# The up projection of a 512-token block as seven products of quarters instead of eight, with the sums of weight quarters made beforehand in DRAM

## The reference, cut to what matters

```python
D_MODEL, SEQ, D_FF = 1024, 512, 4096
def first_block(x, ...):
    ...
    x = x + y @ w_out[l]
    xn2 = rmsnorm(x, norm2_g[l])
    x = x + jnp.square(jax.nn.relu(xn2 @ w_up[l])) @ w_down[l]
    return x
```

## Time and profile before

| | |
|---|---|
| median of 3 runs | 1969.43 us (1969.37 to 1969.91) |
| span of the profiled execution, first to last instruction | 1967.4 us |
| PE busy | 1959.2 us, 9686 matmuls |
| PE weight loads busy | 1614.8 us, 9686 |
| DVE busy | 1024.1 us |
| ACT busy | 764.9 us |
| POOL busy | 83.8 us |
| DMA | 183.36 MB, mean 93 GB/s |

### The profile page before, as it was taken

How to read it: one execution, slowest core, us unless ns; L and a number is a source line. 1 busy time by engine, 2 the same in 40 slices (tenths; PEclk the granted TensorE clock), 3 DMA queues, 4 the chain that set the end, 5 groups by cost and what they waited for, 6 DMA issues and landing times.

```text
span 1967.4 us, 23153 instructions
## 1 busy us (share of the span) xinstructions
PE 1959.2 (100%) x9686; PEld 1614.8 (82%) x9686; DVE 1024.1 (52%) x1394; ACT 764.9 (39%) x1226; POOL 83.8 (4%) x132
## 2 busy tenths in 40 slices
PE   9999999999999999999999999999999999999998
PEld 8888888888888888888888888888888888887776
DVE  5553466435453436643334355545554447596675
ACT  5556563332323333442134232222222321447864
POOL 0000000000000000000000000000000000005541
PEclk9999999999999999999999999999999999999999
DMA  6222222223122242233233323232323334521011
GB/s 214 84 68 85 65 86 75 86 91 106 65 91 86 87 148 86 86 107 108 86 105 89 106 86 107 86 107 89 105 86 107 86 124 114 152 81 44 23 55 65
DMA packets 184295, 183.36 MB, mean 93 GB/s; under 512 B 5120, under 2 KB 159232, under 8 KB 184192
## 3 DMA queue, kind: packets, MB, share of 16 engines
q1 hardware_dynamic: 179840, 172.15, 28.2%
q10 hardware_dynamic: 4352, 9.75, 1.6%
HBM read 175.59 MB, written 4.19 MB: 91 GB/s over the span
## 4 chain that ended last, share of the span: by engine, by line
PE 98%; ACT 1%; DVE 0%; DMA 0%; issue 0%; POOL 0%; DVEq 0%; ACTq 0%
PE bank L1403 85%; PE bank L1630 2%; PE bank L1611 2%; PE bank L1644 2%; PE bank L1501 1%; PE bank L1490 1%; PE bank L1529 1%; PE bank L1413 1%; ACT raw L1663 0%; PE bank L1464 0%; PE bank L1433 0%; PE bank L1509 0%; PE bank L1577 0%; PE bank L1446 0%; PE bank L1620 0%; PE bank L1431 0%
## 5 line engine op out<-in xcount | busy, mean ns | idle before, releaser
L1403 PE MATMUL bank<-xh,wh 128*128 128x512 f32 x1352 | 534.1, 395 | 0.0
L1403 PE MATMUL bank<-xh,wl 128*128 128x512 f32 x1352 | 527.6, 390 | 0.0
L1403 PE MATMUL bank<-xl,wh 128*128 128x512 f32 x1352 | 527.0, 390 | 0.0
L1680 ACT CAST wh<-raw 128x2048 fp32r<-128x2048 f32 (+2 forms) x151 | 279.5, 1854 | 408.8 <-PE bank L1403 405.1
L2234 DVE TENSOR_TENSOR wl<-raw,wh 128x2048 fp32r<-128x2048 f32 (+2 forms) x151 | 335.0, 2221 | 169.5 <-ACT wh L1680 169.3
L1403 PEld LDWEIGHTS bank<-xh,wl 128*128 128x128 f32 x1352 | 253.4, 187 | 53.8
L1403 PEld LDWEIGHTS bank<-xh,wh 128*128 128x128 f32 x1352 | 253.7, 188 | 50.3
L1403 PEld LDWEIGHTS bank<-xl,wh 128*128 128x128 f32 x1352 | 253.8, 188 | 50.0
L1403 PE MATMUL bank<-wh,xh 128*128 128x512 f32 x320 | 129.4, 404 | 0.0
L1403 PE MATMUL bank<-wh,xl 128*128 128x512 f32 x320 | 125.1, 391 | 0.0
L1403 PE MATMUL bank<-wl,xh 128*128 128x512 f32 x320 | 125.1, 391 | 0.0
(11 more groups left out here) (325 smaller groups left out, 2925.8 us busy)
## 6 DMA issues: line engine op xcount, KB each, us to landing
raw<-in_w_in SPq DMA_DIRECT2D x49, 1024.0 KB, 5.0
raw<-in_a_w_in SPq DMA_DIRECT2D x32, 1024.0 KB, 5.5
raw<-in_w_up SPq DMA_DIRECT2D x16, 1024.0 KB, 5.3
raw<-in_w_down SPq DMA_DIRECT2D x16, 1024.0 KB, 5.8
raw<-in_w_proj_b SPq DMA_DIRECT2D x8, 1024.0 KB, 5.1
raw<-in_a_w_out SPq DMA_DIRECT2D x8, 1024.0 KB, 5.7
raw<-in_w_out SPq DMA_DIRECT2D x4, 1024.0 KB, 5.2
raw<-in_w_kv SPq DMA_DIRECT2D x4, 1024.0 KB, 4.9
```

The lines of the kernel that those rows point to most:

```text
L1403: m = e.matmul(o, p, q, start=k == 0 and n == 0, stop=k == K - 1 and n == 2)
L1680: m = e.copy(hi, r)
```

## The change

**Seven products.** The work is cut into 8 groups (`f` 0 or 1, `g` 0 to 3) of 512 features. In a group the contraction is cut in two halves of 512 inputs, the features in two of 256 and the tokens in two of 256. The block product of 2 by 2 by 2 quarters has eight quarter products; here it is formed from seven, of sums of weight quarters and sums of activation quarters. A product (`seven`) is 2 feature blocks x 4 input blocks x 3 matmuls, each 128x128 stationary by 128x256 moving. Products 1, 6, 5 and 3 add up in one bank, `st12`; 2 has the bank `st11`; 7 and 4 share `st21`. On the way ScalarE copies `st12` to a `tmp` three times (`shot`, behind products 1, 6 and 5) and VectorE adds or subtracts the other bank (`piece_sum`); four pieces of 256 features by 256 tokens (two blocks of 128 features) come out. `SEVENS` is the order of the 28 products of a half.

**Weights.** Of seven weight operands three are plain quarters of `w_up`, four are sums. The sums lie in a new DRAM tensor `sums` (8 x 4 blocks of 128x1024). Pool makes them with 64 DMAs of 512 KB: 32 copies, 32 accumulating ones (`accum_op=ALU.add`), issued from the time when the first query tile is done, at most four in flight (four semaphores), each accumulation behind its copy. Loads for the products are 512 KB into halves of the `raw` buffers, six in all; splits (`part`) go to halves of the split buffers, four in all.

**Activations.** The four plain quarters and three sums of quarters of x are made in the stage of `w_out`, by VectorE in the buffer `between`; the sums that have no place in `xh`, `xl` go to the new tiles `xeh`, `xel`.

```diff
+SEVENS = [(0, 1), (1, 1), (2, 1), (0, 2), (1, 2), (0, 7), (1, 7), (0, 6), (1, 6), (0, 5), (1, 5), (0, 3), (0, 4),
+          (1, 3), (1, 4), (3, 1), (2, 2), (3, 2), (2, 7), (3, 7), (2, 6), (3, 6), (2, 5), (3, 5), (2, 3), (2, 4),
+          (3, 3), (3, 4)]
...
+def sevens(f):
+    out, low = [], []
+    for i, (g, n) in enumerate(SEVENS):
+        out.append(("seven", f, g, n))
+        if f == 0 and i == ROOT[1]:
+            out += [("sum_squares", 1), ("root", 1)]
+        out += low
+        if n in (2, 6, 5):
+            out.append(("shot", f, g, 1 if n == 2 else n))
+        if n in PIECE_OF:
+            out.append(("piece_sum", f, g, PIECE_OF[n]))
+        out += after_chunk(("seven", f, g, n))
+        if n in PIECE_OF:
+            out.append(("piece", f, g, PIECE_OF[n]))
+        low = [("piece_low", f, g, PIECE_OF[n])] if n in PIECE_OF else []
+    return out + low
...
-ROOT = {1: 5, 2: 4, 3: 0}
+ROOT = {1: 2, 2: 4, 3: 0}
...
+        def seven(f, g, n):
...
+            w.wait_ge(*told("lo", ("seven", f, g, n)))
+            hi, lo = split_half(("seven", f, g, n))
+            for t in range(2):
+                for k in range(4):
...
+                    for x, (p, q) in enumerate(((hi, h), (hi, l), (lo, h))):
+                        m = e.matmul(bank[:, t * 256:(t + 1) * 256], p[:, c], q,
...
         def wo(c, j):
-            add_x(("wo", c, j), c * 2 + j, 1, "norm2_g")
+            k = c * 2 + j
+            t, v = tmp[2 + k % 3], between[:, k % 2, :]
+            add_x(("wo", c, j), k, 1, "norm2_g")
...
+            if k < 4:
+                e.tensor_tensor(v[:, 0:256], t[:, 0:256], t[:, 256:512], ALU.subtract).then_inc(*tell("x_sum", k))
...
+            stt(v[:, 0:256], xT[:, k - 4, 256:512], v_("norm2_g", k - 4), t[:, 256:512], ALU.mult, ALU.subtract).then_inc(
+                *tell("x_sum", k, "x_less"))
...
+            stt(v[:, 256:512], xT[:, k - 4, 0:256], minus_g[:, k - 4:k - 3], v[:, 0:256], ALU.mult, ALU.add).then_inc(
+                *tell("x_sum", k, "x_least"))
...
+            e.tensor_tensor(v[:, 512:768], t[:, 0:256], v[:, 256:512], ALU.add).then_inc(*tell("x_sum", k))
...
+        def sum_weights(q, n, step):
+            j, other = SUM_STEPS.index((q, n, step)), MADE_OF[n][step]
+            if j >= 4:
+                w.wait_ge(*told(f"sum{j % 4}", *SUM_STEPS[j - 4]))
+            if step:
+                w.wait_ge(*told(sum_of(q, n, 0), q, n, 0))
...
+            if step:
+                e.dma_start(sum_block(n, q), added(other, q), accum_op=ALU.add, max_dma_last_dim=4096).then_inc(
+                    *tell(sum_of(q, n, step), q, n, step, by=16))
+            else:
+                e.dma_start(sum_block(n, q), added(other, q)).then_inc(*tell(sum_of(q, n, step), q, n, step, by=16))
+
+        w.wait_ge(*told("tile", ("q", 0, 3)))
+        for each in SUM_STEPS:
+            sum_weights(*each)
         follow("pool", rate)
```

More of the change, by code:

```diff
@@ L158, in lay_out @@
     for f in range(2):
[L159 to L162, removed]
+        for g, n in SEVENS:
+            if n in SUM_OF:
+                chunk(("seven", f, g, n), SUM_OF[n], f * 4 + g, 4, 0, 256, "sum")
+            else:
+                chunk(("seven", f, g, n), "w_up", 512 * (n != 1), 4, f * 2048 + g * 512 + 256 * (n == 4), 256, "quarter")
         for c in range(8):
@@ L222, in after_chunk @@
 def after_chunk(name):
[L224 to L228, removed]
+    out = []
+    for new in AFTER.get(name, []):
+        if new[0] == "seven":
+            out.append(("part", *new[1:]))
+        elif new in PIECES:
+            out += [("w_piece", new, x) for x in range(4)]
+        elif name not in LATE and new not in PIECED:
+            out.append(("w", NTH[new]))
+    return out
 LATE = (("vsw", 0), ("vsw", 1))
-PIECES = (("wo", 1), ("up", 0, 2))
+PIECES = (("wo", 1),)
 PIECED = (("q", 0, 1), ("bo", 0, 0), ("bo", 0, 1), ("bo", 1, 0), ("bo", 1, 1), *PIECES)
@@ L272, in summed @@
     o = whole(key)
-    split = [t for t in o if k == 7 and t[0] in ("w", "w_piece")]
+    split = [t for t in o if k == 7 and t[0] in ("w", "w_piece", "part")]
     return [t for t in o if t not in split] + squared(s, k) + split
@@ L423, in some @@
             for x in t:
-                if x[0] == "mm" and ends_chunk(*x[1:]) and AFTER[ends_chunk(*x[1:])] in PIECED:
-                    pieces.extend(("w_piece", AFTER[ends_chunk(*x[1:])], y) for y in range(4))
+                if x[0] == "mm" and ends_chunk(*x[1:]):
+                    pieces.extend(("w_piece", new, y) for new in AFTER.get(ends_chunk(*x[1:]), ()) if new in PIECED for y in range(4))
         del fill[:n]
@@ L1685, in w_piece, with part, shot, piece @@
             w.wait_ge(*told(f"raw{SLOT[n]}", n))
-            if name in BEFORE:
-                w.wait_ge(*told(*chunk_read(BEFORE[name])))
+            for old in BEFORE.get(name, ()):
+                w.wait_ge(*told(*chunk_read(old)))
             c = slice(x * 512, x * 512 + 512)
             e.copy(wh[WSLOT[name]][:, c], raw[SLOT[n]][:, c]).then_inc(*tell("hi", name, x))
+        def part(f, g, n):
+            name = "seven", f, g, n
+            w.wait_ge(*told(f"half{SLOT[PLACE[name]]}", name))
+            for old in BEFORE[name]:
+                w.wait_ge(*told(*chunk_read(old)))
+            e.copy(split_half(name)[0], raw_half(name)).then_inc(*tell("hi", name))
+        def shot(f, g, n):
+            piece = SHOT[n]
+            w.wait_ge(*told("tile", ("seven", f, g, n)))
+            if piece_before(f, g, piece):
+                w.wait_ge(*told("hl", *piece_before(f, g, piece)))
+            elif piece == "11":
+                w.wait_ge(*told("xl", 1, 6 + g, "sums"))
+            else:
+                w.wait_ge(*(told("sum_square", 1, 7) if piece == "21" else told("ssq", 1)))
+            e.copy(shot_place(g, piece)[:, :], bank_of("st12", ("st", f, g, "12"))[:, :]).then_inc(*tell("shot", f, g, n))
+        def piece(f, g, c):
+            t = shot_place(g, c)
+            w.wait_ge(*(told("st_out", f, g, c) if c == "12" else told("st_out", f, g, c, "relu")))
+            act(t[:, :], t[:, :], ACT.Square).then_inc(*tell("up_sq", f, g, c))
+            if f:
+                w.wait_ge(*told("tile", ("down", 0, 7, 0)))
+            else:
+                after("mix")
+            w.wait_ge(*told("up_sq", f, g, c))
+            e.copy(h_part(hh, g, c), two(t[:, :])).then_inc(*tell("hh", f, g, c))
         def w_part(k):
@@ L2904, in sync @@
             slot = SLOT[n]
-            if slot in SLOT[:n]:
-                old = CHUNKS[max(x for x in range(n) if SLOT[x] == slot)]
-                w.wait_ge(*(told("w1", *old[0][1:]) if old[6] == "whole" else told("lo", old[0], 3) if old[0] in PIECED else told("lo", old[0])))
-            m = a[matrix]
+            for old in RAW_BEFORE[n]:
+                w.wait_ge(*told(*raw_free(old)))
+            m = None if kind == "sum" else a[matrix]
             if n == 0:
```

349 lines of the change are left out of this document (235 added, 114 removed).

## The result

The changed kernel took 1973.5 us (median of 13 runs, 1972.4 to 1974.0) against 1969.4 for the kernel before (13 runs on the same chip): ratio 1.0019, 95% interval 1.0011 to 1.0028. The prediction was 1957.4, range 1950 to 1967. The multiplications did become cheaper, and more than all of it went elsewhere.

The account below looks back on a forecast made before the run. TensorE was taken as the bound, fed without a gap: span 1967.4 - 16.1 (products) + 3.5 (start) + 0.6 (borders) = 1955.4 us; with the median 2.0 above the span, 1957.4, range 1950 to 1967.

Parts of the forecast that it names:

- Part 1: Up stages: 1344 matmuls of 256 columns at 117.5 ns replace 768 of 512 at 226.6, a gain of 16.1 us.
- the range that I gave: Start-to-start time of the products' matmuls: bounds 113.3 to 126.7 ns; the forecast's own range had 114 to 121.
- Part 2: Start of the first up stage: PE waits 3.5 us for the third product's weights, queued on DVE behind the last x block.
- late by 1.7, and by 1.0 at the last block: DVE's lateness in us on x blocks during `w_out`, from two weight halves split in the sixth block.
- 16.8: Start of the first up stage: reciprocal finished 16.8 us after `w_out` ends; seventh product's weights at 18.0, due at 20.8.
- The upper bound of 7: Largest wait in us allowed at the third product, if each hand-over costs 0.2 us more.
- Borders: End of each half, where the down stage's full chunk must be split: 0.3 us on each of the two.
- Part 3: Steady state of the products: DVE 82% and ACT 72% busy, lateness absorbed by halves split ahead; cost 0.
- The lockstep rival: ACT and DVE alternating in runs of pieces make PE wait: 12 us in all, time 1969; milder 4 us, 1961; 15%.
- Parts 4 and 5: Weight loads for the products stay hidden, and Pool's 64 DMAs for sums in DRAM finish in time; cost 0 each.
- the 14.3 from which they would have decided: Average us per Pool DMA above which late weight sums would hold up the products; 23 for the first 32.
- late sums: Rival: Sync stands at the first summed half's load, PE at the sixth product; at 16 us per DMA, 2070 us; 9%.

Follow-up runs that it names:

- run 4: The changed kernel, with all but the first matmul of each group of twelve taking 128 columns instead of 256: 2029.1 us in one run.
- run 2: The changed kernel, with the ring of five PSUM banks moved on by two ahead of the second down stage: 1965.9 us.
- run 3: The changed kernel, with the third and fourth products' weights prepared ahead of the last x block, the fifth's behind it, then the sum of squares: 1971.2 us.
- run 5: run 3, with two bank copies and the ninth and tenth products' weight parts moved forward, two of these steps ahead of the reciprocal: 1970.0 us.
- run 9: run 6, with the copy of the ninth product's bank and the eleventh product's weight part moved ahead of the second piece: 1960.3 us, ratio 0.9952.
- run 1: The changed kernel, with the ring of five PSUM banks moved on by two at the first conv tile: 1967.4 us.
- run 8: The kernel before, without products or sums, with its ring of banks moved on by three at the first conv tile: 1976.5 us, ratio 1.0036.
- run 6: The changed kernel with the order of run 5 and the ring steps of run 2 together: 1963.0 us, ratio 0.9967.
- run 7: run 6, with the ring moved on by one ahead of `w_out` and by one ahead of the second down stage: 1964.2 us.

## Why the prediction was wrong, point by point

- **Part 1, 117.5 ns.** Measured 120.0 from the third matmul on. The rows that I took it from are groups of six, in which starts stand 116 to 119 ns apart; in the long stream of the up stages nearly all stand at 120.0, and over 1344 matmuls 2.5 ns are 3.4 us. It lies in the range that I gave, and run 4 fits what was said of it ("256 columns is close to the width at which loading takes over"): half the columns save 8 ns. 120.0 and 226.6 both leave 13.3 ns beyond their columns at 2.4 GHz, and I had the second number: 106.7 + 13.3 was to be had from the earlier trace rows. The Trainium skill ("TensorE: Matmul & The Clock Gate", Back-to-back issue gap) has 2.5 ns beyond the columns, 109.2, and says that this is the gap of a single matmul by itself. The measured 120.0 does not agree with it.
- **Part 2, the start, 3.5 us.** Place, releaser and row were right; the size was 6.3, and 2.2 more at the lower clock. The failed step is "late by 1.7, and by 1.0 at the last block", which puts the last addition 1.2 us behind the end of `w_out`: it came 3.9 us behind. A late block takes DVE 5.08 us and not 4.75, since it waits 0.30 for ACT's cast of 768 each time, and a full chunk is split at 798.7 just ahead (2.3 us), which I had not in the queue. From the addition on, 7.9 us were reckoned and 8.0 measured (819.16 to 827.15). That idle time costs clock was no term at all: 6.3 us cost 8.5 in this trace. The upper bound of 7 was too low for it. For the reciprocal, 12.5 + 3.35 is 15.9 and not the 16.8 that stands there; nothing hung on it, since the seventh product did not wait.
- **Borders, 0.3 us each.** The weights' share was right: 0.53 us between starts at the first, where 0.12 is the pitch. The second was 1.74, by the ring's bank (run 2).
- **Part 3, steady state, 0.** Right. From 833 us to the last product of each half no two starts on PE are over 0.3 us apart; DVE is at 78 and 73% in the two stages, ACT at 64 and 62%. The lockstep rival, with waits in each run of pieces, is out. But the first stage's zero was measured behind a start that came 8.5 us late. With that delay taken away, PE waited 3.1 us at the ninth product (run 3) or 2.1 at the eleventh (run 5), until the order was put right for these as well (run 9): as I read it, that delay had given DVE and ACT time, which the sum did not count on.
- **Parts 4 and 5, loads and sums, 0.** Right, although much happened there. Pool's row on the page ends in the fifth slice, some 245 us, long before 700. In 30 to 240 us, issues with us from issue to landing:

```profile
sums<-in_w_up POOLq DMA_DIRECT2D x48, 512.0 KB, 9.7
raw<-in_w_in SPq DMA_DIRECT2D x16, 1024.0 KB, 11.5
sums<-sums POOLq DMA_DIRECT2D x16, 512.0 KB, 6.9
```

  The 64 take 3 us each in passing, far below the 14.3 from which they would have decided. Weight loads beside them take 11.5 us and not 5.1, and PE does not see it: its waits hold no landing.
- **The term that was missing**, the ring of banks at nothing, is the step that failed most and the largest: 6.5 us at 1671 in the trace, of which 4.0 are the wait and the rest slow matmuls behind it (6.2 by the median of run 1, 7.2 by that of run 8). I followed every queue that the change touches, and not the counter that its 32 missing tiles no longer moved. "The remaining work is unchanged" was in the sum without being written down. It is this term that carried the time out of the range: run 2, the change with the ring's phase put right, took 1965.9, within 1950 to 1967.

The sum, in span: -16.1 + 3.4 (pitch) + 8.5 (start) + 2.0 (borders) = -2.2, where -1.8 was measured at 1671; with 6.5 that is +4.7. The rival that ended slower (late sums) was a wrong mechanism; the right one was not among them, and 9% for "slower" was too little for a change that alters what hands out buffers to the whole rest of the program.

## What to carry to other kernels

When a change takes tiles out of a round-robin pool, or gives them a pool of their own, every later tile of that pool moves: compare the phase (count of takes modulo the number of buffers) before and after, and look far behind the edit for a reader that was late all along and harmless in its old place. When one wait at a crowded start is taken away, the next one in the same queues appears; go through the order of the queue product by product before expecting the full size (here 6.3 us of gap became 4.5, 3.5 and 1.6 over three orders). A wait of PE of 3 us or more cost more than itself here, since slow matmuls came behind it; by how much differed from one execution to the next.

## What the runs showed of the hardware

- TensorE's clock: a gap of 6.4 us was followed by 4.8 us at 213 ns per 256-column matmul (1.2 GHz) in the change, and by fewer such matmuls in runs 1 and 2 (13 and 11 against 21). A gap of 3.4 us (run 3) was followed by full speed until 844.7, 1.4 us after the restart, and then some 3 us at the lower level. Gaps of 1.3 us were followed by full speed. So was a gap of 2.4 us in runs 5 and 6, but in run 7 by 16 matmuls at the lower level, from 849.2 on. With 128-column matmuls behind a gap of 6.8 us the lower level stayed for 138 us (827.4 to 965.8, run 4).
- Executions of one kernel differ by the granted clock: in run 6 the three of 1962.0 to 1962.7 us show a mean of 0.999, the three of 1963.3 to 1963.7 us one of 0.998.
- Matmuls of 128, 256 and 512 columns, each with its weight load: 112, 120.0 and 226.6 ns from start to start.
- Copies and accumulating copies inside DRAM from Pool, 0.52 MB each, up to four in flight: 9.7 us where the source is the weight matrix, 6.9 where it is a packed sum; beside them all 16 DMA engines are 96% busy at 241 GB/s, and 1 MB loads take over twice as long. The Trainium skill ("SBUF — State Buffer", SBUF: two separate sides) has Pool's descriptor writing held up by DVE's two-port operations. DVE was 47% busy in that stretch, and whether part of the 9.7 us is that, no run here shows.
